# Last expert pair of layer 1: sent rows added ahead of w3, w2 tiles loaded and multiplied in halves

## Chip, cores and metric

The kernel runs on one core of a Trainium2 chip. The metric is the device time of one execution in microseconds (us); lower is better. Three runs of the kernel before the change took 819.95, 822.08 and 824.09 us, median 822.08 us.

## What is computed

One step of a two-layer network on 256 tokens (128 of a prompt, 128 of a sample) of width 1024, all in float32. What matters here is the mixture of experts that ends each layer, and that of layer 1 above all, which ends the program but for a final norm:

```python
def hierarchical_moe(h, w_grp, w_exp, w1, w3, w2):      # 16 experts, two for each token
    ...                                                 # gate: the token's weight for each expert
    hg = jnp.einsum('td,edf->tef', t, w1)               # w1, w3: 1024 x 512 for each expert
    hu = jnp.einsum('td,edf->tef', t, w3)
    a = jax.nn.silu(hg) * hu * gate[..., None].astype(t.dtype)
    y = jnp.einsum('tef,efd->td', a, w2)                # w2: 512 x 1024
    return y.reshape(b, n, d)
# then x = x + gate2 * y, and after layer 1 the outputs are rmsnorm(x, final_g)
```

## The kernel before

**Pairs of experts.** The 16 experts of a layer are taken in `PAIRS` = 8 pairs, i = 0 to 7. The rows that were routed to a pair are gathered, up to `CAP` = 64 for each expert, so that one matmul instruction for expert 2i fills output partitions 0 to 63 and one for expert 2i+1 fills 64 to 127; two such instructions run side by side. On TensorE (`compact` of the tensor block) a pair goes: w1 into PSUM bank 6, w3 into bank 7, the product silu(w1) * w3 made by VectorE (line 1747), four 128x128 transposes of it (line 807), the transposed halves copied back to SBUF by ScalarE (line 1202, `hidT_lo`) and VectorE (line 1756, `hidT_hi`), and w2 into banks 4 and 5. w2 runs with h, the half of the 1024 output columns, outside and f, the four blocks of 128 of the hidden size, inside.

**Where a pair's output goes.** In layer 1 the first `SENT` = 6 pairs are sent: their rows are scaled by the gate and scattered by GpSimd into a DRAM buffer `yrows` (line 1417), which holds two rows of 4 KB for each token. After pair 5's rows are sent, GpSimd loads `yrows` back (line 1455) with four transfers of 512 KB each, in the order group 0 first copy, group 0 second copy, group 1 first copy, group 1 second copy; the two of group g raise the semaphore `y_back[g]`. They land in the SBUF place of the tile ("w3", 1, 13), pair 6's, as soon as TensorE is done with it. VectorE adds the two copies of a group (`sum_sent(g)`, line 1710), and TensorE adds the sum to the accumulators in PSUM banks 0 to 3 by eight 128x128 matmuls against the identity (`add_sent(g)`, 16 records in the trace, as each float32 matmul is recorded as two). Pairs 6 and 7 aren't sent; their w2 output is multiplied with a scatter matrix into the same accumulators (16 records of 128x256).

**The end of pair 7 before the change.** TensorE's order is w1, w3, `add_sent(0)`, the transposes, `add_sent(1)`, w2, scatter. VectorE's order is `spread` (line 1731), `sum_sent(0)`, the product (line 1747, two halves), `sum_sent(1)`, `hidT_hi`, and the copy of the second half of the output (line 1769). Each engine runs its list in order, so an instruction that waits holds back all behind it. After the scatter come the residual, the final norm, the transposes back and the stores.

**Weights.** An expert's w1, w3 or w2 is one tile of 2 MB, 16 KB contiguous for each of 128 partitions. SyncE issues the loads in one fixed order on one queue (line 480), each as soon as the place is free, into nine places (six of `ring`, and `spare`, `bench`, `back`). For pair 7: w1 goes to a ring place and `back`, w3 to `spare` and `bench`, w2 to two ring places. The `yrows` loads go on GpSimd's queue, and both queues share the same transfer engines.

Of the kernel before, what the change touches and what calls it, by code (L numbers as in the profile page):

```python
# [29 lines left out]
FC = FF // P  # L30
# [33 lines left out]
CAP = 64  # L64
# [81 lines left out]
def backbone(nc, x_prompt, x_sample, cache_k, cache_v, c, c_ctx, w_ada, b_ada, norm_mix_g, norm_ffn_g,  # L146
# [3 lines left out]
    with ExitStack() as ctx:  # L150
# [3 lines left out]
        def sem(name):  # L154
            return ctx.enter_context(nc.semaphore(name))
# [125 lines left out]
        icnt = cst[:, C_CNT:C_CNT + 4 * P].rearrange("p (w t) -> p w t", w=4)  # L281

        slot_full = [sem(f"slot_full{s}") for s in range(SLOTS + 3)]
        tiles_used = sem("tiles_used")
        s_x = sem("s_x")
        s_cst = sem("s_cst")
# [124 lines left out]
        def landed(eng, key):  # L411

            n = TILE[key]
            eng.wait_ge(slot_full[SLOT[n]], 16 * TURN[n])
# [25 lines left out]
        def is_sent(l, i, r):  # L440

            return l == 1 and r == 0 and i < SENT

        def ysel_count(l, i, r):

            n = i + l * PAIRS
            return 2 * n - (min(i, SENT) if l == 1 and r == 0 else 0)
# [6 lines left out]
        @block.sync  # L454
        def _(sp):
            def load(key):
                n = TILE[key]
                src = SOURCE[key[0]](key[1], key[2])
                rows, width = src.shape
                dst = place(n)[:, 0:rows // P * width].rearrange("p (k n) -> p k n", k=rows // P)  # L460
                if BEFORE[n] is not None:
                    sp.wait_ge(tiles_used, BEFORE[n] + 1)
                sp.dma_start(dst, src.rearrange("(k p) n -> p k n", p=P)).then_inc(slot_full[SLOT[n]], 16)  # L463

            for g, x in enumerate((x_prompt, x_sample)):
                sp.dma_start(xtok[:, g, :], x[0]).then_inc(s_x, 16)

            sp.wait_ge(small_issued, 2)
            for key in STREAM[:TILE["w1", 0, 0]]:
                load(key)  # L470

            def load_experts(l):
                first = TILE["w1", l, 0]

                def expert_tile(i, t, expert):

                    n = first + SLOTS * i + t
                    dst = place(n).rearrange("p (k n) -> p k n", k=FC if t >= 4 else DC)
                    src = (moe_w1, moe_w3, moe_w2)[t // 2][l, expert].rearrange("(p k) n -> p k n", p=P)
                    sp.dma_start(dst, src).then_inc(slot_full[SLOT[n]], 16)  # L480

                for i in range(PAIRS):
                    for t in range(SLOTS):
                        n = first + SLOTS * i + t
                        if BEFORE[n] is not None:
                            sp.wait_ge(tiles_used, BEFORE[n] + 1)
                        elif SLOT[n] == BENCH and l == 0:

                            sp.wait_ge(pv_done, 1)
                            sp.wait_ge(s_out, 32)  # L490
                        elif SLOT[n] == SPARE:

                            sp.wait_ge(pool_done, 1)
                        elif SLOT[n] == BENCH:

                            sp.wait_ge(dconv_done, len(PE_CHUNKS))
                        else:

                            sp.wait_ge(htok_ready, 4 * l + 4)
                        expert_tile(i, t, 2 * i + t % 2)  # L500

            load_experts(0)
            for key in STREAM[TILE["w2", 0, NE - 1] + 1:TILE["w1", 1, 0]]:
                load(key)
            load_experts(1)
            for g, y in enumerate((y_prompt, y_sample)):
                for h in range(2):
                    sp.wait_ge(out_ready[2 * g + h], 1)
                    sp.dma_start(y[0][:, h * TW:(h + 1) * TW], xtok[:, g, h * TW:(h + 1) * TW]).then_inc(s_out, 16)

            sp.wait_ge(s_out, 96)
# [3 lines left out]
        def _(pe):  # L515
# [202 lines left out]
            def tile_landed(l, i, j):  # L718

                landed(pe, STREAM[TILE["w1", l, 0] + SLOTS * i + j])  # L720

            def gather(which, i, half):

# [28 lines left out]
            def compact(l, i, r):  # L752
# [5 lines left out]
                for w, bank, j in ((w1, 6, 0), (w3, 7, 2)):  # L758
                    tile_landed(l, i, j)
                    tile_landed(l, i, j + 1)  # L760
                    if j == 0:

                        pe.wait_ge(hsel_lo[r], n + 1)
                        pe.wait_ge(mod_taken, (6, 9)[l])
                    else:

                        pe.wait_ge(spread_ready[r], n + 1)
                    for k in range(DC):
                        if j == 0 and k == 4:

                            pe.wait_ge(hsel_hi[r], n + 1)
                            pe.wait_ge(pick_ready[r], n + 1)
                            for g in range(2):
                                if is_sent(l, i, r):
                                    last = mm(ps[:, 7, 0:4].rearrange("p (s u) -> p s u", s=2), pick[i % 2][:, g, :],
                                              send[:, g, :, 2 * i:2 * i + 2], g == 0, g == 1)
                                else:
                                    last = nc.tensor.transpose(ps[:, 7, g * TG:(g + 1) * TG], pick_gate[:, g, :], ident)  # L778
                            last.then_inc(spread_done[r], 1)
                        for u in range(2):  # L780
                            c = slice(CAP * u, CAP * u + CAP)
                            last = mm(ps[c, bank, :], hsel[:, k, c], w[u][:, k, :], k == 0, k == DC - 1)
                        if k == 0 and j == 2 and r == 0:

                            pe.wait_ge(hid_done[r], n * 2 + 1)
                            pe.sem_inc(tiles_used, 2)
                    last.then_inc(hid_done[r], 1)

                if ahead:

                    pe.wait_ge(rows_in, 16 * (i + l * FETCHED + 1))
                    pe.wait_ge(ysel_lo[0], n)
                    turn_rows(0)
                    if i + 2 < PAIRS:
                        pe.wait_ge(ysel_hi[0], n)
                        locate(l, i + 2, ps[:, 5, 0:1])
                elif r == 0 and l == 1:
                    add_sent(0)
                for f in range(FC):
                    if f == 2 and r == 0:  # L800

# [9 lines left out]
                if ahead:  # L811

                    pe.wait_ge(at_ready, min(i + 2, FETCHED) + l * FETCHED)
                    pe.wait_ge(ysel_hi[0], n)
                    turn_rows(1)
                elif r == 0 and l == 1:
                    add_sent(1)
                tile_landed(l, i, 4)
                tile_landed(l, i, 5)
                for h in range(2):  # L820
                    if ahead:

                        pe.wait_ge((hsel_lo, hsel_hi)[h][0], n + 2)
                    for f in range(FC):
                        if h == 0 and f % 2 == 0:

                            pe.wait_ge((hidT_lo[r], hidT_hi[r])[f // 2], n + 1)
                        for u in range(2):
                            c = slice(CAP * u, CAP * u + CAP)
                            last = mm(ps[c, 4 + h, :], hidT[:, f, c], w2[u][:, f, h * 512:(h + 1) * 512],  # L830
                                      f == 0, f == FC - 1)
                    if h == 0 or not is_sent(l, i, r):
                        last.then_inc(ysel_done[r], 1)
                    else:

                        last.then_inc(tiles_used, 2)
# [52 lines left out]
            def crowded(l, i):  # L889

                n = i + l * PAIRS
                with nc.body(f"pe_crowded_{n}", parent=pe_at[n], valid_engines=[mybir.EngineType.PE]):

                    pe.wait_ge(ysel_lo[0], n)
                    pe.wait_ge(ysel_hi[0], n)
                    way = pe.value_load(path[0:1, i:i + 1], min_val=0, max_val=2)
                    with pe.If(way == 1):
                        pe.wait_ge(more_ready, n + 1)
# [560 lines left out]
        def _(dve):  # L1459
# [247 lines left out]
            def sum_sent(g):  # L1707

                dve.wait_ge(y_back[g], 32)
                V.tensor_tensor(back_rows[:, 0, g, :], back_rows[:, 0, g, :], back_rows[:, 1, g, :],  # L1710
                                ALU.add).then_inc(y_summed, 1)

            def compact(l, i, r):
# [26 lines left out]

                if l == 1 and r == 0 and i == PAIRS - 1:
                    sum_sent(0)
                dve.wait_ge(sil_ready[r], n + 1)
                dve.wait_ge(hid_done[r], n * 2 + 2)
                for h in range(2):
# [4 lines left out]
                                    ALU.mult).then_inc(hid_ready[r], 1)  # L1750
                if r == 0 and i + 2 < PAIRS:
                    take_at(l, i + 2, ps[:, 5, 0:1])
                if l == 1 and r == 0 and i == PAIRS - 1:
                    sum_sent(1)
                dve.wait_ge(turn_done[r], n * 2 + 2)
                V.tensor_copy(hidT[:, 2:4, :], ps[:, 7, 0:2 * P].rearrange("p (f j) -> p f j", f=2)).then_inc(
                    hidT_hi[r], 1)
# [268 lines left out]
```

## Time and profile before

| | us |
|---|---|
| median of 3 runs | 822.08 |
| span of the profiled execution, first to last instruction | 821.7 |
| TensorE busy in it | 760.8 (93%) |
| VectorE / ScalarE / GpSimd busy | 235.0 / 165.6 / 50.2 |
| HBM read | 285.63 MB, 358 GB/s over the span |

The profile gives no time for the profiled execution beyond its span, which is 0.4 us under the median of the runs. The chain that ended last is TensorE for 75% of the span and DMA for 16%. Times below are us from the span's start. "issue" before a matmul is time in which the profile shows no releaser for the wait; a matmul that waits for a weight tile can appear so.

### The profile page before, as it was taken

The page shows a single profiled execution, that of the slowest core. Times are in us where ns is not written, and L with a number is a line of the kernel's source. Part 1 is how long each engine was busy: PE and PEld are TensorE (multiplying, and loading weights), DVE is VectorE, ACT ScalarE, POOL GpSimd, SP SyncE. Part 2 cuts the span into 40 slices and gives each one's busy share as a digit, 9 for nine tenths or more (in the row PEclk, how much of TensorE's full clock was granted, in tenths as well). Part 3 has the DMA queues.
Part 4 walks back from the last instruction along what each step waited for, and adds up shares of the span by engine and source line. Part 5 has one row for each costly group of instructions (what it writes and reads, how often), then busy time and mean ns, then how long its engine had stood idle before and what let it go on. Part 6 is the DMA issues. An engine that isn't in the chain of part 4 may idle for free.

```text
span 821.7 us, 10485 instructions
## 1 busy us (share of the span) xinstructions
PE 760.8 (93%) x4071; PEld 426.7 (52%) x4071; DVE 235.0 (29%) x667; ACT 165.6 (20%) x373; POOL 50.2 (6%) x74
## 2 busy tenths in 40 slices
PE   4699889999999999999799999999998989999796
PEld 4387458754344434443488758683334353333344
DVE  2301331531111111011779931451211112121115
ACT  3210420330100010001502862451010000110012
POOL 5023000010000000000100000001000000001000
PEclk9899999889999999999999999969998999999988
DMA  9997999879999999999995259577999909999941
GB/s 293 400 398 256 412 409 430 345 284 427 424 427 426 426 429 425 426 427 413 398 399 228 108 216 429 194 298 313 430 422 424 392 18 424 428 428 427 419 172 55
DMA packets 42643, 289.67 MB, mean 353 GB/s; under 512 B 4418, under 2 KB 5902, under 8 KB 30291
## 3 DMA queue, kind: packets, MB, share of 16 engines
q1 hardware_dynamic: 36752, 275.78, 81.9%
q0 software_dynamic: 5056, 11.98, 3.9%
q10 hardware_dynamic: 770, 1.06, 0.4%
q8 instruction: 39, 0.64, 0.3%
q14 instruction: 26, 0.21, 0.1%
HBM read 285.63 MB, written 8.52 MB: 358 GB/s over the span
## 4 chain that ended last, share of the span: by engine, by line
PE 75%; DMA 16%; issue 3%; DVE 3%; ACT 1%; SPq 1%; POOL 1%; PEld 0%; DVEq 0%; PEldq 0%; POOLq 0%
PE ps L517 71%; DMA ring<-in_conv_w 4%; DMA back<-in_moe_w 4%; DMA spare<-in_moe_w 3%; DMA ring<-in_w_in_ab 3%; DMA ring<-in_w_ada 3%; DVE work L1747 1%; SPq L463 1%; PE ps L939 1%; PE ps L807 1%; PE ps L741 1%; DVE rstd L1484 0%; PE ps L778 0%; POOL work L1365 0%; PE ps L669 0%
## 5 line engine op out<-in xcount | busy, mean ns | idle before, releaser
L517 PE MATMUL ps<-ring,work 128*64 128x512 f32 x1088 | 304.5, 595 | 3.0 <-issue 2.0
L517 PEld LDWEIGHTS ps<-ring,work 128*64 128x64 f32 x1088 | 94.6, 137 | 144.9 <-issue 144.8
L517 PE MATMUL ps<-back,ring 128*128 128x256 f32 x656 | 148.3, 388 | 6.3 <-DMA ring<-in_conv_w 2.6
L517 PEld LDWEIGHTS ps<-back,ring 128*128 128x128 f32 x656 | 125.7, 194 | 28.1 <-issue 4.2
L517 PE MATMUL ps<-bench,work 128*64 128x512 f32 x208 | 96.1, 611 | 2.0 <-DVE work L1704 1.4
L517 PE MATMUL ps<-spare,work 128*64 128x512 f32 x176 | 80.4, 611 | 4.7 <-issue 4.7
L517 PE MATMUL ps<-back,work 128*64 128x512 f32 x160 | 72.0, 597 | 0.0
L1747 DVE TENSOR_TENSOR work<-work,ps 128x256 f32<-128x256 f32 x34 | 19.4, 611 | 162.9 <-PE ps L517 162.9
L517 PE MATMUL ps<-ring,csil 128*32 128x512 f32 x352 | 44.4, 633 | 8.1 <-DMA ring<-in_w_ada 8.1
L1911 DVE SCALAR_TENSOR_TENSOR work<-work,dw 128x256 f32<-128x256 f32 x120 | 50.8, 479 | 1.0
L1198 ACT ACTIVATE work<-ps 128x512 f32<-128x512 f32 x17 | 10.1, 597 | 200.8 <-PE ps L517 200.8
L517 PEld LDWEIGHTS ps<-bench,work 128*64 128x64 f32 x208 | 27.8, 140 | 29.0 <-issue 28.7
L517 PEld LDWEIGHTS ps<-spare,work 128*64 128x64 f32 x176 | 24.3, 141 | 34.3 <-issue 34.3
L517 PE MATMUL ps<-work 128*128 128x256 f32 x176 | 40.9, 386 | 0.0
L517 PEld LDWEIGHTS ps<-work 128*128 128x128 f32 x176 | 32.6, 190 | 12.9 <-issue 8.9
L1191 ACT ACTIVATE work<-ps 128x512 f32<-128x512 f32 x18 | 10.8, 597 | 121.6 <-PE ps L741 97.0
L1431 POOL DMA_INDIRECT part<-hbuf,row_at x14 | 14.4, 1026 | 298.4 <-PE ps L741 274.6
L517 PE MATMUL ps<-work,xtok 128*128 128x128 f32 x128 | 22.1, 346 | 8.2 <-issue 5.1
L517 PEld LDWEIGHTS ps<-back,work 128*64 128x64 f32 x160 | 20.8, 137 | 16.7 <-issue 16.7
L1769 DVE COPY work<-ps 128x512 f32<-128x512 f32 x11 | 7.6, 691 | 74.3 <-PE ps L517 74.3
L517 PEld LDWEIGHTS ps<-ring,csil 128*32 128x32 f32 x352 | 11.9, 113 | 32.0 <-issue 19.5
L517 PE MATMUL ps<-back,ones 128*128 128x256 f32 x96 | 24.6, 408 | 3.8 <-ACT back L1111 2.2
(238 smaller groups left out, 636.4 us busy)
## 6 DMA issues: line engine op xcount, KB each, us to landing
ring<-in_moe_w SPq DMA_DIRECT2D x63, 2048.0 KB, 19.3
ring<-in_w_ada SPq DMA_DIRECT2D x22, 2048.0 KB, 18.3
bench<-in_moe_w SPq DMA_DIRECT2D x12, 2048.0 KB, 20.5
spare<-in_moe_w SPq DMA_DIRECT2D x11, 2048.0 KB, 20.6
back<-in_moe_w SPq DMA_DIRECT2D x10, 2048.0 KB, 21.8
ring<-in_conv_w SPq DMA_DIRECT2D x6, 2048.0 KB, 24.3
ring<-in_w_in_ab SPq DMA_DIRECT2D x2, 2048.0 KB, 25.0
ring<-in_w_out_ab SPq DMA_DIRECT2D x2, 2048.0 KB, 21.2
```

Of the source, the lines that this page charges most:

```text
L463: sp.dma_start(dst, src.rearrange("(k p) n -> p k n", p=P)).then_inc(slot_full[SLOT[n]], 16)
L517: return nc.tensor.matmul(out, lhsT, rhs, start=start, stop=stop, skip_group_check=True)
L741: last = nc.tensor.transpose(ps[:, 4 + half, (k % 4) * P:(k % 4 + 1) * P], hrows[:, k * P:(k + 1) * P], ident)
L807: last = nc.tensor.transpose(ps[:, 6 + f // 2, (f % 2) * P:(f % 2 + 1) * P], hid[:, f * P:(f + 1) * P], ident)
L939: last = nc.tensor.transpose(ps[:, 2 * g + k // 4, (k % 4) * P:(k % 4 + 1) * P], hT[:, k, g * TG:(g + 1) * TG], ident)
L1191: nc.scalar.activation(hsel[:, 0:4, :], ps[:, 4, :].rearrange("p (k j) -> p k j", k=4), ACT.Copy).then_inc(hsel_lo[which], 1)
L1198: nc.scalar.activation(sil, ps[:, 6, :], ACT.Silu).then_inc(sil_ready[r], 1)
L1431: nc.gpsimd.indirect_dma_start(hrows, None, hbuf[l], IndirectOffsetOnAxis(ap=row_at[:, 0:1], axis=0), bounds_check=NT - 1, oob_is_err=Fals ...
L1747: V.tensor_tensor(hid[:, h * 2 * P:(h + 1) * 2 * P].rearrange("s (f p) -> s f p", f=2), sil.rearrange("s (p f) -> s f p", f=FC)[:, f, :], ...
L1769: V.tensor_copy(ysel[:, 512:1024], ps[:, 5, :]).then_inc(ysel_hi[r], 1)
L1911: V.scalar_tensor_tensor(out=cv[k], in0=upad[:, k, :, t:t + TG], scalar=dw[:, k, t:t + 1], in1=cv[k], op0=ALU.mult, op1=ALU.add).then_inc( ...
```

## The change

- `w2` of pair 7 of layer 1 is loaded as two half tiles each: the first half (f = 0, 1) of both tiles with semaphores of their own (`front_full`), then the second halves, four transfers of 1 MB in place of two of 2 MB. Each partition's piece is 8 KB.
- `w2` of that pair is multiplied with f outside and h inside: f = 0 and 1 wait for the first halves only, f = 2 for the second. The number of matmuls is the same; both halves h of the output are now complete only in the last of the four blocks f.
- `add_sent(0)` and `add_sent(1)` stand right behind w1, ahead of w3, on TensorE; `sum_sent(1)` stands right behind `sum_sent(0)` on VectorE, ahead of the product.
- Two waits are added to the `crowded` branch, which no pair takes in this trace.

```diff
-                def expert_tile(i, t, expert):
+                def expert_tile(i, t, expert, half=None):
...
+                    if half is None:
+                        sp.dma_start(dst, src).then_inc(slot_full[SLOT[n]], 16)
+                    else:
+                        f = slice(half * FC // 2, (half + 1) * FC // 2)
+                        sp.dma_start(dst[:, f, :], src[:, f, :]).then_inc(
+                            slot_full[SLOT[n]] if half else front_full[t - 4], 16)
...
-                        expert_tile(i, t, 2 * i + t % 2)
+                        expert_tile(i, t, 2 * i + t % 2, 0 if in_halves(l, i) and t >= 4 else None)
+                    if in_halves(l, i):
+                        for t in (4, 5):
+                            expert_tile(i, t, 2 * i + t % 2, 1)
...
                     last.then_inc(hid_done[r], 1)
+                    if j == 0 and r == 0 and l == 1 and not ahead:
+                        add_sent(0)
+                        add_sent(1)
...
-                elif r == 0 and l == 1:
-                    add_sent(0)
...
-                elif r == 0 and l == 1:
-                    add_sent(1)
-                tile_landed(l, i, 4)
-                tile_landed(l, i, 5)
-                for h in range(2):
+                if in_halves(l, i):
+
+                    for f in range(FC):
+                        if f % 2 == 0:
+                            pe.wait_ge((hidT_lo[r], hidT_hi[r])[f // 2], n + 1)
+                        for u in range(2):
+                            if f == 0:
+                                pe.wait_ge(front_full[u], 16)
+                            elif f == FC // 2:
+                                tile_landed(l, i, 4 + u)
+                        for h in range(2):
+                            for u in range(2):
+                                c = slice(CAP * u, CAP * u + CAP)
+                                last = mm(ps[c, 4 + h, :], hidT[:, f, c], w2[u][:, f, h * 512:(h + 1) * 512],
+                                          f == 0, f == FC - 1)
+                            if f == FC - 1:
+                                last.then_inc(ysel_done[r], 1)
+                else:
+                    tile_landed(l, i, 4)
+                    tile_landed(l, i, 5)
+                for h in () if in_halves(l, i) else range(2):
...
                 if l == 1 and r == 0 and i == PAIRS - 1:
                     sum_sent(0)
+                    sum_sent(1)
...
-                if l == 1 and r == 0 and i == PAIRS - 1:
-                    sum_sent(1)
```

## Rows read from the trace of the kernel before

**Rows 1.** Chain of waits from 735 us: start, us, what.
```profile
739.15 29.88 DMA back<-in_moe_w
...
773.15 3.58 PE ps L517 x16
776.73 4.75 issue
781.48 11.81 PE ps L517 x48
```

**Rows 2.** Windows: stretch, length, busy us of each engine (records), TensorE clock, DMA, GB/s.
```profile
776.80:781.40 4.60, 0.00 (x0) 0.00 (x0) 0.00 (x0) 0.57 (x1) 0.00 (x0) 0.87 1.01 427
781.40:787.00 5.60, 5.52 (x14) 1.91 (x16) 0.00 (x0) 0.00 (x0) 0.00 (x0) 0.50 1.03 434
787.00:791.30 4.30, 4.30 (x21) 1.31 (x17) 0.00 (x0) 0.00 (x0) 0.00 (x0) 1.00 0.42 179
```

**Rows 3.** Weight loads of pair 7: SyncE issues (timeline), KB and us to landing (DMA view).
```profile
747.56 0.33 SPq L480 DMA_DIRECT2D bench<-in_moe_w  x1
bench<-in_moe_w SPq DMA_DIRECT2D x1, 2048.0 KB, 33.8
755.42 0.33 SPq L480 DMA_DIRECT2D ring<-in_moe_w  x1
ring<-in_moe_w SPq DMA_DIRECT2D x1, 2048.0 KB, 36.3
```

**Rows 4.** The four `yrows` loads: issues, landing of all four, median of the last two.
```profile
755.69 2.17 POOL L1455 DMA_DIRECT2D ring<-yrows  x4 [13.86 <-PEq L803]
DMA to landing us min/median/max: 10.6/20.0/28.8
ring<-yrows POOLq DMA_DIRECT2D x2, 512.0 KB, 26.0
```

**Rows 5.** Timeline of the sums on VectorE, the second add and w3's end on TensorE.
```profile
773.60 1.22 DVE L1710 TENSOR_TENSOR ring<-ring 128x1024 f32<-128x1024 f32 x1
792.48 1.22 DVE L1710 TENSOR_TENSOR ring<-ring 128x1024 f32<-128x1024 f32 x1
793.85 2.02 PE L517 MATMUL ps<-cst,ring 128*128 128x128 f32 x16
790.70 0.59 PE L517 MATMUL ps<-spare,work 128*64 128x512 f32 x1
```

**Rows 6.** Queues: packets, MB, share from 766 to 772; packets of the whole page.
```profile
q1 hardware_dynamic: 139, 2.03, 80.1%
q0 software_dynamic: 138, 0.50, 21.0%
...
DMA packets 42643, 289.67 MB, mean 353 GB/s; under 512 B 4418, under 2 KB 5902, under 8 KB 30291
```

**Rows 7.** Matmuls at full and half clock (timeline), and a stretch at half clock (windows).
```profile
757.39 7.09 PE L517 MATMUL ps<-ring,work 128*64 128x512 f32 x32 [0.65 <-issue]
782.36 1.06 PE L517 MATMUL ps<-spare,work 128*64 128x512 f32 x1
783.21 1.06 PE L517 MATMUL ps<-spare,work 128*64 128x512 f32 x1
538.97 3.65 PE L939 MATMUL ps<-cst,back 128*128 128x128 f32 x16
39.50:43.00 3.50, 3.38 (x8) 2.76 (x9) 0.00 (x0) 3.50 (x13) 0.00 (x0) 0.51 1.05 384
```

**Rows 8.** Pair 6 between w3 and w2 (timeline): VectorE's product, ScalarE's copy.
```profile
754.67 1.14 DVE L1747 TENSOR_TENSOR work<-work,ps 128x256 f32<-128x256 f32 x2 [10.55 <-PE ps L517]
755.82 0.38 ACT L1202 ACTIVATE work<-ps 128x256 f32<-128x256 f32 x1
```

**Rows 9.** Pair 7's output (timeline): ScalarE's first copy, TensorE's scatter.
```profile
799.50 0.60 ACT L1212 ACTIVATE work<-ps 128x512 f32<-128x512 f32 x1 [5.58 <-PE ps L517]
802.82 3.72 PE L517 MATMUL ps<-work 128*128 128x256 f32 x16
```

More of the change, by code:

```diff
@@ L283, in backbone @@
         slot_full = [sem(f"slot_full{s}") for s in range(SLOTS + 3)]
+        front_full = [sem(f"front_full{u}") for u in range(2)]
         tiles_used = sem("tiles_used")
@@ L442, in is_sent, with in_halves @@
             return l == 1 and r == 0 and i < SENT
+        def in_halves(l, i):
+            return l == 1 and i == PAIRS - 1
         def ysel_count(l, i, r):
@@ L479, in expert_tile @@
                     src = (moe_w1, moe_w3, moe_w2)[t // 2][l, expert].rearrange("(p k) n -> p k n", p=P)
-                    sp.dma_start(dst, src).then_inc(slot_full[SLOT[n]], 16)
+                    if half is None:
[4 more added lines that the diff above has]
+                            slot_full[SLOT[n]] if half else front_full[t - 4], 16)
                 for i in range(PAIRS):
@@ L720, in tile_landed @@
                 landed(pe, STREAM[TILE["w1", l, 0] + SLOTS * i + j])
+                if in_halves(l, i) and j >= 4:
+                    pe.wait_ge(front_full[j - 4], 16)
             def gather(which, i, half):
@@ L895, in crowded @@
                     pe.wait_ge(ysel_hi[0], n)
+                    pe.wait_ge(hsel_lo[0], n + 1)
+                    pe.wait_ge(hsel_hi[0], n + 1)
                     way = pe.value_load(path[0:1, i:i + 1], min_val=0, max_val=2)
```

## The prediction, made before the changed kernel was run

> **What bounds the kernel now.** I read the chain of waits first, since the change touches only the last pair. There the reader sees four facts [rows 1]. TensorE's w1 of pair 7 starts when the tile in `back` lands at 739.15 + 29.88 = 769.03; it ends at 773.15 + 3.58 = 776.73; then TensorE stands for 4.75 us; from 781.48 it runs without a stop worth naming to the end of w2. The chain calls the 4.75 us "issue", so I looked up what w3 needs: its second tile goes to `bench`, issued at 747.56 and landed 33.8 us later, at 781.36 [rows 3]. So w3 starts 0.12 us after its weights are home, and the stall is a transfer, not TensorE.
>
> The windows view shows a second cost of that stall [rows 2]. The transfer engines are full through it (427 GB/s, then 434), so nothing loads faster by being asked for earlier. And the granted clock falls in it: the mean is 0.87 over the idle stretch and 0.50, the 1.2 GHz level, from 781.40 to 787.00, then 1.00 again, 2.4 GHz. w3 therefore runs its first 5.5 us at half clock and ends at 790.70 + 0.59 = 791.29 [rows 5], 9.8 us after its start, where 32 records of the same shape took 7.09 us in pair 6 at full clock [rows 7].
>
> w2 is not held by its weights. Its last tile was issued at 755.42 and landed 36.3 us later, at 791.7 [rows 3]; w2 starts where `add_sent(1)` ends, at 793.85 + 2.02 = 795.87 less the overlap of pipelined matmuls, 795.80. Between w3's end and w2's start lie 4.5 us, of which two adds of some 2 us each are the larger part.
>
> **The sent rows decide.** The adds can go into the 4.75 us stall only if their data are there. VectorE's first sum starts at 773.60, so group 0 is home by then. Of group 1 the kernel before tells nothing by a wait, since its sum comes at 792.48 [rows 5]. The DMA view does. Four loads are issued from 755.69 on, over 2.17 us, so at about 755.7, 756.2, 756.8 and 757.3; the first lands after 10.6 us, the last after 28.8, and the last two have a median of 26.0, so 23.2 for the third [rows 4]. That puts the landings at 766.3, about 773.1, 780.0 and 786.1. `y_back[1]` needs the fourth: **786.1, some 4.7 us after w3's weights**. After the change TensorE may not start w3 before it has added group 1.
>
> **Part by part.**
>
> *`add_sent(0)` ahead of w3.* Its sum ends at 773.60 + 1.22 = 774.8, before w1 ends. It runs from about 776.8 to 778.8, in a stall that exists anyway: nothing on the path.
>
> *The second sum and `add_sent(1)` ahead of w3.* VectorE waits for the fourth load; queued behind it there are only the product and the copies, which need w3 anyway. Does the fourth load land when it did? From 766 to 772 the two queues moved 139 and 138 packets, with 2.03 and 0.50 MB [rows 6]: packet for packet, where a packet of GpSimd's queue is mostly one 4 KB row. On SyncE's queue it is a whole 16 KB partition: the page counts 42643 - 30291 = 12352 packets of 8 KB and more, and 96 expert tiles of 128 partitions are 12288 [rows 6]. The change halves the packets of w2, the tiles that follow `bench` at 781.4, so one turn of both queues is 8 + 4 = 12 KB in place of 20, 0.6 of the time. At 781.4 the fourth load has had 1.4 of its 6.1 us (780.0 to 786.1); 0.77 x 6.1 x 0.6 = 2.8 us more give 784.2, and with the 6.8 us that the transfers before it took, 784.7. I take 784.4. Bounds: 783.7 if the whole load runs beside halves (6.1 x 0.6), 786.1 if the queues share by bytes and nothing changes.
>
> The Trainium skill, page "DMA: Bandwidth & Descriptors", section "Queues, rings and completion order", says that a transfer engine takes turns between its queues packet by packet. The counts of 139 and 138 agree; by that rule the fourth load comes early, as I take it, and without it the sum would be that of rival 1.
>
> Then 1.22 us of sum and about 0.15 to start TensorE, as from 792.48 + 1.22 = 793.70 to 793.85 [rows 5]: it starts at 785.8, after 7 us of idling. A stall of 4.75 us took the clock to half [rows 2], so `add_sent(1)` runs at half clock. Sixteen such 128x128 records at half clock took 3.65 us [rows 7], at full 2.02 [rows 5]; I take 3.7, and w3 starts at 789.5. The full-clock price would need a stall without a fall, which no row here shows for 7 us.
>
> *w3.* It started at 781.48, so it is 8.0 us late. Part comes back: the half clock lasted 5.5 us from the restart [rows 2], and if it does so again it ends at 791.3. A pair of records costs 0.85 us at half clock (782.36 to 783.21) and 7.09 / 16 = 0.44 at full, 0.43 without the tail of the last [rows 7]. The 1.8 us from 789.5 take 2.1 of the 16 pairs, 13.9 x 0.43 = 6.0 the rest, and 0.16 the last one's tail: w3 ends at 797.4, 6.1 later than 791.3. The half clock is bounded below by 3.5 us, a stretch after an earlier stall that ran at a mean of 0.51 throughout [rows 7], and above by a longer one, as the next restart may fall differently: -0.9 and +0.6 us.
>
> *From w3 to w2.* With the adds gone, the way is that of pair 6: product at 754.67, ScalarE's copy ends at 755.82 + 0.38 = 756.20 [rows 8], 0.05 for TensorE to see it, and the product itself starts 0.1 after w3's end; together 1.75 us in place of 4.5. **This returns 2.75.** `hidT_hi` is done some 0.6 us after w2's start and is asked for only at f = 2, half of 7.0 us later.
>
> *w2 in halves.* Now w2 starts at 799.2. Both tiles were home at 791.7 and the bytes are the same, so the halves, front and back, are home some 7 us before they are needed: loading and multiplying by halves gives nothing on this path, and the two further issues on SyncE hide behind a queue that is full. The matmuls are the same in number and shape, 795.80 to 802.82, 7.0 us. It costs a little: h = 0 is complete only in the last block f, 0.86 us before the end, where ScalarE's copy used to run at 799.50, 3.3 us before the scatter [rows 9]. The copy takes 0.60, so about 0.1 us shows.
>
> *Sum.* 797.4 + 1.75 + 7.0 + 0.1 = 806.3 for the scatter's start in place of 802.82: **+3.5 us**. All behind it stays. The profiled execution would go from 821.7 to 825.2; the median of the runs lies 0.4 above the span, so I predict **825.6 us** (+0.4%). Checked the other way: 6.1 - 2.75 + 0.1 = 3.5.
>
> **Rivals.**
>
> 1. *Shares by bytes.* If packets of half the size change nothing, the fourth load lands at 786.1, TensorE restarts at 787.5, and all is 1.7 us later: +5.2, 827.3. For it: only whole tiles are shown in the trace. Against it: the even packet counts.
>
> 2. *The rows come in time, and the change is faster.* If the fourth load were home by 781.48 - 2.0 - 0.15 - 1.22 = 778.1, both adds would fill the stall; if the clock then stays up, w3 would take 781.48 to 788.5, and the scatter would start at 788.5 + 1.75 + 7.1 = 797.4: -5.4, 816.7. The point of no gain is a landing at 780.9. For it: the landings are read from the DMA view alone, and nothing in the kernel before waits for the fourth. Against it: the third lands at 780.0 and four times 0.5 MB at the pace of rows 6 cannot come sooner.
>
> 3. *A short half clock.* If it lasts 3.5 us from the restart, w3 runs at full clock: -0.9, 824.7. If the clock doesn't fall at all, add and w3 cost 1.7 and 0.9 less, 823.0.
>
> 4. *The change doesn't do what it says:* that w2 is bound by its load and the halves free it. The row of the last tile (791.7 against 795.80) speaks against it; it would matter only in rival 2, where w2 would start at 790.3 and need its second half at 793.8, still later than 791.7.
>
> **How the numbers follow.** Forecast 0.53, rival 1 0.21, rival 2 0.12, rival 3 0.14; rival 4 has no time of its own. The forecast's own range is 824.7 to 826.9. The range reaches from rival 3's lower time, less 1 us since three runs of one kernel spread by 4 us, to rival 1 and 0.7 above it: 822.0 to 828.0, which leaves out rival 2 and some tails. A measurement of this kernel can tell about 0.5%, 4.1 us, from no change; slower by more starts at 826.2, within the forecast's range. Slower: rival 1 and a third of the forecast, 0.39. Faster: 0.12 and a little for noise, 0.13. Same: 0.48.
>
> **What would show it.** Right: in the changed profile the second sum on VectorE starts at about 784.4, long after the first; `add_sent(1)` starts at about 785.8 with 16 records over some 3.7 us at clock 0.50; w3 starts at about 789.5, though its weights land at 781.4 as before; from w3's end to w2's start there are 1.75 us; the page counts about 256 packets more. The load's landing tells the forecast (784.4) from rival 1 (786.1). Wrong: a second sum before 781, w3 starting with its weights, or w2 waiting for its halves.

## The result: 0.65% slower, and the profile after

The changed kernel took 827.57 us (median of 14 runs, 823.36 to 829.56) against 822.15 of the kernel before it: ratio 1.0065, 95% interval 1.005 to 1.0081. That is slower, by 5.4 us where 4.1 were called measurable; the interval begins just at that half per cent. The time is inside the predicted range (822.0 to 828.0) and 2 us above the predicted 825.6. Here and below ratios use fast runs alone, as a few executions (one of 1122 us among them) fall into a slower state, and they need not be the exact quotient of the two medians.

The page of the changed kernel: span, and packets of all queues.

```profile
span 827.4 us, 10490 instructions
DMA packets 42931, 289.68 MB, mean 350 GB/s; under 512 B 4449, under 2 KB 5933, under 8 KB 30322
```

Its span is 5.7 us longer than before's 821.7. The profiled execution took 829.29 us, 1.9 above its span and 1.7 above the median; in the profiled runs of the experiments, too, the time lies 1.8 to 1.9 us above the span, so before's profile, too, is of an execution slower than its median (estimate: 823.5 us). The page counts 288 packets more than before [rows 6]; 256 of them are the halves.

Pair 7 in the timeline of the changed kernel (start, us, engine, line, tiles out<-in, count, and in brackets the idle time before it with its releaser): w1's first matmul, the two sums on VectorE with the adds on TensorE, w3's first and last, the product, w2, the scatter.

```profile
772.90 0.61 PE L530 MATMUL ps<-ring,work 128*64 128x512 f32 x1 [1.14 <-DMA back<-in_moe_w]
...
777.38 1.22 DVE L1744 TENSOR_TENSOR ring<-ring 128x1024 f32<-128x1024 f32 x1
...
780.44 2.05 PE L530 MATMUL ps<-cst,ring 128*128 128x128 f32 x16
787.13 1.22 DVE L1744 TENSOR_TENSOR ring<-ring 128x1024 f32<-128x1024 f32 x1 [8.54 <-DMA ring<-yrows]
788.50 3.75 PE L530 MATMUL ps<-cst,ring 128*128 128x128 f32 x16 [6.01 <-DVE ring L1744]
792.19 1.05 PE L530 MATMUL ps<-spare,work 128*64 128x512 f32 x1
...
799.08 0.59 PE L530 MATMUL ps<-spare,work 128*64 128x512 f32 x1
799.80 1.12 DVE L1782 TENSOR_TENSOR work<-work,ps 128x256 f32<-128x256 f32 x2 [11.45 <-PE ps L530]
801.37 7.09 PE L530 MATMUL ps<-ring,work 128*64 128x512 f32 x32
808.39 3.72 PE L530 MATMUL ps<-work 128*128 128x256 f32 x16
```

The stall before w3 is now named: TensorE idles 6.01 us for VectorE's second sum, and VectorE had idled 8.54 us for `yrows`. The DMA view (first line: KB and us from issue to landing) and the view of the loads' own line (second) put w3's own weights ahead of that:

```profile
bench<-in_moe_w SPq DMA_DIRECT2D x1, 2048.0 KB, 33.9
...
DMA to landing us min/median/max: 10.7/20.0/26.4
```

The tile in `bench` was issued at 751.21 and landed 33.9 us later, at 785.1. The second line is that of the four `yrows` loads, issued from 759.1 to 760.7: the fourth landed 26.4 us after its issue, at 787.1, just when the second sum starts. TensorE takes w3 up only at 792.19, 7.1 us after w3's weights are home. The clock in the windows view of that stretch (third column from the right), before, in and after the restart:

```profile
784.00:786.00 2.00, 0.00 (x0) 0.00 (x0) 0.00 (x0) 0.00 (x0) 0.00 (x0) 1.00 1.03 422
786.00:788.00 2.00, 0.00 (x0) 0.00 (x0) 0.86 (x1) 0.00 (x0) 0.00 (x0) 0.55 1.00 414
788.00:790.00 2.00, 1.50 (x7) 1.53 (x8) 0.36 (x1) 0.00 (x0) 0.00 (x0) 0.50 1.02 426
790.00:792.00 2.00, 2.00 (x11) 1.96 (x10) 0.00 (x0) 0.00 (x0) 0.00 (x0) 0.50 1.01 422
792.00:794.00 2.00, 2.00 (x10) 0.64 (x10) 0.00 (x0) 0.00 (x0) 0.00 (x0) 0.74 0.74 311
```

The add runs at 1.2 GHz, 3.7 us where the first add took 2.05, and w3 at 2.4 GHz from about 793.0 on.

**Where the 5.7 us lie.** I split each profile at w1 of pair 7 and at the scatter, and call what lies between them the tail. Before: 769.13 to 802.82, 33.69 us. After: 772.90 to 808.39, 35.49 us. So the tail gives only 1.8 of the 5.7; 3.8 were lost before w1 of pair 7, where the prediction had put nothing; 0.1 lies behind the scatter. The split is that of two single executions.

**An error in what stands ahead of the prediction.** There I wrote that no pair takes the `crowded` branch, to which the change adds two waits. That is wrong: TensorE's first matmuls of pair 3 of layer 1 in the trace of before (timeline) lie in it. They gather that pair's rows, once at 627 and once at 662 us:

```profile
627.48 4.84 PE L517 MATMUL ps<-work,xtok 128*128 128x128 f32 x21 [3.40 <-issue]
632.75 1.70 PE L517 MATMUL ps<-work,xtok 128*128 128x128 f32 x11 [0.43 <-issue]
...
662.69 3.81 PE L517 MATMUL ps<-work,xtok 128*128 128x128 f32 x32 [1.32 <-issue]
```

The same in the kernel after:

```profile
626.93 3.35 PE L530 MATMUL ps<-work,xtok 128*128 128x128 f32 x14 [3.38 <-issue]
631.56 4.00 PE L530 MATMUL ps<-work,xtok 128*128 128x128 f32 x18 [1.28 <-issue]
...
665.63 5.44 PE L530 MATMUL ps<-work,xtok 128*128 128x128 f32 x32 [2.90 <-issue]
```

From the first gather to w1 of pair 7 it is 141.65 us before and 145.97 after. The second gather alone is idle 1.6 us longer and takes 1.6 longer. The prediction has no term for any of this.

### The profile page after: what moved, and what is told of

Same layout as the page of the kernel before. It is cut to its first block, busy times and chain, and to the rows that moved or that the text cites. A ratio compares the mean times of both kernels' runs of the same rounds, so it can differ in the third digit from the quotient of the medians.

```text
span 827.4 us, 10490 instructions
## 1 busy us (share of the span) xinstructions
PE 766.5 (93%) x4071; PEld 432.2 (52%) x4071; DVE 235.3 (28%) x667; ACT 165.8 (20%) x373; POOL 50.2 (6%) x74
## 4 chain that ended last, share of the span: by engine, by line
PE 78%; DMA 12%; DVE 3%; issue 3%; POOL 1%; ACT 1%; SPq 1%; PEld 0%; DVEq 0%; PEldq 0%; POOLq 0%
PE ps L530 74%; DMA ring<-in_conv_w 4%; DMA ring<-yrows 3%; DMA ring<-in_w_in_ab 3%; DMA ring<-in_w_ada 3%; DVE work L1782 1%; PE ps L973 1%; SPq L468 1%; PE ps L823 1%; PE ps L756 1%; PE ps L793 0%; DVE rstd L1518 0%; POOL work L1399 0%; PE ps L682 0%; DVE back L1980 0%
## 5 line engine op out<-in xcount | busy, mean ns | idle before, releaser
L530 PE MATMUL ps<-bench,work 128*64 128x512 f32 x208 | 94.0, 599 | 1.5 <-DVE work L1738 1.4
L530 PE MATMUL ps<-spare,work 128*64 128x512 f32 x176 | 78.0, 596 | 0.0
L530 PE MATMUL ps<-work,xtok 128*128 128x128 f32 x128 | 24.9, 376 | 10.6 <-issue 7.6
L530 PEld LDWEIGHTS ps<-work,xtok 128*128 128x128 f32 x128 | 23.6, 285 | 12.1 <-issue 12.1
L530 PEld LDWEIGHTS ps<-back,work 128*64 128x64 f32 x160 | 20.8, 137 | 16.7 <-issue 16.7
```

What stands on the lines that cost most here:

```text
L530: return nc.tensor.matmul(out, lhsT, rhs, start=start, stop=stop, skip_group_check=True)
```

## The experiments

There were three theories to tell apart; more than one can hold. **A**: the cost is in pair 7, because group 1's rows land after w3's weights and TensorE has to add them first. **B**: the two waits in the `crowded` branch cost time by being executed. **C**: code that is longer shifts the branch's instructions, and the branch, entered by a jump, is fetched worse from its new place. A fourth question was whether the halves of w2 do anything. Times below are medians, each run with the kernel before on the same chip (three chips in all), and ratios are to that kernel.

**Each part alone.** `adds_only` is the kernel before with sums and adds moved ahead, w2 whole, no new waits:

```diff
                     last.then_inc(hid_done[r], 1)
+                    if j == 0 and r == 0 and l == 1 and not ahead:
+                        add_sent(0)
+                        add_sent(1)
...
-                elif r == 0 and l == 1:
-                    add_sent(0)
...
-                elif r == 0 and l == 1:
-                    add_sent(1)
...
                     sum_sent(0)
+                    sum_sent(1)
...
-                if l == 1 and r == 0 and i == PAIRS - 1:
-                    sum_sent(1)
```

> Both adds and both sums ahead, w2 loaded and multiplied whole, no added waits. The sums wait for the last load of the sent rows. My prediction's theory (queues share packet for packet, so halves of w2 bring that load 1.7 us sooner): here it lands 30.4 us after the first of the four was issued, as before, so the time is 1.7 us above the changed kernel's end of pair 7. From w1's start to the scatter's start before 33.7 us, after 35.5; here 37 to 38.5. Rival (shares by bytes): 35.5 as after, landing 28.0 us after the first issue. Time of the whole: 825 to 829; by theory B of the waits run it is free of the branch's cost, so under 827.

It took 826.95 us, ratio 1.0059 (1.0032 to 1.0086). `halves_only` is the kernel after with the opposite edit to this one and without the two waits:

```diff
-                        add_sent(0)
-                        add_sent(1)
...
+                elif r == 0 and l == 1:
+                    add_sent(0)
...
+                elif r == 0 and l == 1:
+                    add_sent(1)
...
-                    pe.wait_ge(hsel_lo[0], n + 1)
-                    pe.wait_ge(hsel_hi[0], n + 1)
...
-                    sum_sent(1)
...
+                if l == 1 and r == 0 and i == PAIRS - 1:
+                    sum_sent(1)
```

> w2 of pair 7 loaded and multiplied in halves, adds and sums where they were before, no added waits. Prediction: nothing gained, as w2's weights are home 4 us before w2 starts: 33.7 us from w1's start to the scatter's start, 822.2 +- 1. Packet for packet: the last load of the sent rows lands about 28 us after the first was issued (before 30.4); by bytes 30.4. Rival (halves bring something of their own): 821 or less.

It took 824.38 us, ratio 1.0014 (0.9992 to 1.0036). The third is `waits_only`, the kernel before with the waits alone:

```diff
                     pe.wait_ge(ysel_lo[0], n)
                     pe.wait_ge(ysel_hi[0], n)
+                    pe.wait_ge(hsel_lo[0], n + 1)
+                    pe.wait_ge(hsel_hi[0], n + 1)
```

> The kernel before with nothing but the two added waits in the branch for a crowded pair. In the profile of the changed kernel pair 3 of layer 1 goes through that branch, and w1 of pair 7 starts 3.8 us later than in the kernel before (772.90 against 769.13), of which the branch adds most. Theory A (the time is all made in pair 7): 822, no change, and w1 of pair 7 starts at 769 +- 1. Theory B (the branch's code, with its waits or its place in the instruction stream, costs time too): 823 to 826, and the stall ahead of the second gather of pair 3 is 2.9 us as after the change, not 1.3 as before.

It took 824.32 us, ratio 1.0032 (1.0013 to 1.0051). So the loss comes apart into two: the adds' order, 4.8 us by its ratio, and the waits, 2.6, with intervals that overlap; the halves by themselves gain nothing. The profile of `waits_only` shows its loss nowhere: it is of the fastest of its twelve runs (821.60 us), w1 of pair 7 starts at 768.38, and the second gather waits 1.15 us, not the 2.9 that was expected. In `adds_only` (timeline: w1, the second sum, the second add, the scatter) group 1 decides even more, since here w2's packets are whole:

```profile
768.85 0.61 PE L517 MATMUL ps<-ring,work 128*64 128x512 f32 x1 [0.99 <-DMA back<-in_moe_w]
...
785.39 1.22 DVE L1709 TENSOR_TENSOR ring<-ring 128x1024 f32<-128x1024 f32 x1 [10.86 <-DMA ring<-yrows]
786.76 3.75 PE L517 MATMUL ps<-cst,ring 128*128 128x128 f32 x16 [8.33 <-DVE ring L1709]
...
806.79 3.72 PE L517 MATMUL ps<-work 128*128 128x256 f32 x16
```

The tail is 37.94 us, 2.45 longer than that of after. In the view of the loads' line the fourth load lands 28.5 us after its issue here, 28.8 in the kernel before, 26.4 in after and 26.3 in `halves_only`. In all seven kernels that load w2 whole and the rows as before it takes 28.5 to 28.8, in all four with halves 26.3 or 26.4. Here is the line of `adds_only`, then the two queues of the kernel after from 783 to 785 (packets, MB, share of the engines):

```profile
DMA to landing us min/median/max: 10.4/19.7/28.5
```

```profile
q1 hardware_dynamic: 71, 0.56, 66.8%
q0 software_dynamic: 67, 0.27, 33.1%
```

So halves do what the prediction said of packets: they bring the other queue's load home some 2.3 us sooner. Packets of 8 KB and of 4 KB take turns almost one for one, as those of 16 and 4 KB did before [rows 6]. That is the rule of the Trainium skill named there (turns packet by packet), and the counts and the landings agree with it; sharing by bytes would have changed nothing.

**What the prediction costed, exactly.** `no_waits` is the kernel after without the two waits in the branch, so all that the prediction's sum holds and nothing else:

```diff
-                    pe.wait_ge(hsel_lo[0], n + 1)
-                    pe.wait_ge(hsel_hi[0], n + 1)
```

> The changed kernel without the two added waits in the branch for a crowded pair: adds and sums ahead, halves, nothing else. The waits alone cost 2.6 us (ratio 1.0032). Theory B (the branch costs part of the change's time, through its waits): 823.5 to 825, ratio to the kernel before 1.002 to 1.004, and from the first gather of pair 3 to w1 of pair 7 under 144 us (after 146.0, before 141.7). Theory C (the branch's cost comes from where its code lies, which the halves move too): 825 to 828 with a second gather that waits 2.5 to 2.9 us and three instruction fetches around it, as in all kernels with halves so far. From w1's start to the scatter's start in pair 7: 34.4 to 36, as in the changed kernel.

It took 825.96 us against 822.23, ratio 1.0042 (1.0014 to 1.0070): by its ratio +3.5 us, with an interval from 1.2 to 5.8, where the sum said +3.5. Timeline of its second sum, second add and scatter:

```profile
782.34 1.23 DVE L1742 TENSOR_TENSOR ring<-ring 128x1024 f32<-128x1024 f32 x1 [8.67 <-DMA ring<-yrows]
783.71 3.75 PE L530 MATMUL ps<-cst,ring 128*128 128x128 f32 x16 [6.15 <-DVE ring L1742]
...
803.76 3.72 PE L530 MATMUL ps<-work 128*128 128x256 f32 x16
```

With w1 at 767.98 its tail is 35.78, that of after (35.49) within 0.3. Theory A stands for pair 7. That the ratio meets the sum is in part luck: the tail is only 2.1 us longer than before's. The time lies above the 823.5 to 825 expected by theory B, while from the first gather to w1 it is 141.96 us, as B has it.

**Only the first add ahead.** If group 1 is what costs, the change with group 1 left in its old place should keep the gain of `add_sent(0)` in the stall. `first_add` is the kernel after with this edit:

```diff
                         add_sent(0)
-                        add_sent(1)
...
+                elif r == 0 and l == 1:
+                    add_sent(1)
...
                     sum_sent(0)
-                    sum_sent(1)
...
+                if l == 1 and r == 0 and i == PAIRS - 1:
+                    sum_sent(1)
```

> As the changed kernel, but only group 0 is added ahead of w3; group 1 is summed and added where it was before. If the cost is the wait for the last load of the sent rows, w3 starts with its weights again, 12.4 us after w1's start, and one add of 2.05 us has left the way from w3 to w2, so the scatter starts 31.5 to 32 us after w1's start where w3 still runs its first 5.5 us at half clock, and 29 if the clock stays up: 817 to 820.5, plus what the branch costs by theory B. If it is the reordering as such that costs, it stays near 825.

It took 823.90 us, ratio 1.0036 (1.0013 to 1.0058). The loss in the tail is gone, but the expected gain is not there. The timeline shows why:

```profile
782.87 0.90 PE L530 MATMUL ps<-spare,work 128*64 128x512 f32 x1 [2.80 <-issue]
...
791.76 1.12 DVE L1782 TENSOR_TENSOR work<-work,ps 128x256 f32<-128x256 f32 x2 [15.60 <-PE ps L530]
792.80 1.22 DVE L1745 TENSOR_TENSOR ring<-ring 128x1024 f32<-128x1024 f32 x1
794.16 2.02 PE L530 MATMUL ps<-cst,ring 128*128 128x128 f32 x16 [0.79 <-DVE ring L1745]
...
803.13 3.72 PE L530 MATMUL ps<-work 128*128 128x256 f32 x16
```

TensorE's second add waits for VectorE's second sum, and that stands behind the product, as in the kernel before [rows 5]. The first add used to run while VectorE was busy with that; moving it only lengthens TensorE's wait later. From w3's end to w2's start it is 4.5 us, as before. The tail, 32.65 us from w1 at 770.48, misses the 31.5 to 32 expected, though w3 ran only 3.4 us at half clock, and is like that of kernels that leave pair 7's order alone with as short a half clock (last section). The ratio holds the two waits too.

**Waits or place?** Four kernels set B against C. `pad4` and `pad24` are the kernel before with 4 or 24 more waits on a semaphore already raised, at the end of TensorE's main program, ahead of the branch's code; `dead24` has 24 in the branch of layer 0's first pair, which is not taken, so that they shift code and never run; `waits_back` is `waits_only` with 488 in that same branch. The edits of `pad24` and of `dead24`:

```diff
+            for _ in range(24):
+                pe.wait_ge(hsel_lo[0], 1)
             last_bb = nc.cur_bb
             pe.br("pe_end")
```

```diff
+                    for _ in range(24 if n == 0 else 0):
+                        pe.wait_ge(hsel_lo[0], 1)
                     pe.wait_ge(ysel_lo[0], n)
```

> The kernel before with four waits that are long fulfilled put at the end of TensorE's program, ahead of the code of the crowded branches: no new wait in any branch, only their code lies four instructions later. Theory C: the gathers of pair 3 break at another place, the second waits up to 2.9 us and three fetches of instructions lie around it, and the time is 1 to 3 us above the kernel before. If only waits inside the branch cost: no change, 822 +- 1, second gather after 1.2 to 1.6 us.

> As the run before with 24 such waits, as many as the two added waits in each of the twelve branches up to pair 3 of layer 1. Theory C: as the kernel with the waits alone: the first gather breaks after some 15 records, not 21, and the time is 2 to 3 us above the kernel before. If waits inside the branch cost as such: no change, 822 +- 1.5.

> The kernel before with 24 waits in the branch of layer 0's first pair, which isn't taken: nothing more is executed, but the code of all later branches lies as much later as two added waits in each would put it. Where the first gather of pair 3 breaks tells the shift: 21 records before, 15 in the kernel with the waits and in the one with 24 waits at the end. Theory C (place of the code): break after 15, and the time 1.5 to 3 us above the kernel before, as theirs (1.0032 and 1.0025). Theory B (executed waits): break after 15, and no change, 822 +- 1.2.

> The two waits in every branch, and 488 more in the branch that isn't taken, so that the code lies later by some 256 instructions in all; if instructions come in blocks of that many, the first gather breaks after 21 records again. Theory C: with the break back at 21 the time is back at 822 +- 1.2 although the waits are executed. Theory B: the waits still cost 2 to 3 us. If the break is elsewhere, the run tells only that place's time.

Ratios: `pad4` 1.0009 (0.9985 to 1.0034), `pad24` 1.0025 (1.0000 to 1.0050), `dead24` 1.0007 (0.9979 to 1.0035), `waits_back` 1.0018 (0.9992 to 1.0045). The first gather of the branch in `waits_only`, then in `dead24`, then in `waits_back` (timeline):

```profile
625.24 3.56 PE L517 MATMUL ps<-work,xtok 128*128 128x128 f32 x15 [3.56 <-issue]
630.23 3.79 PE L517 MATMUL ps<-work,xtok 128*128 128x128 f32 x17 [1.42 <-issue]
```

```profile
626.57 3.56 PE L517 MATMUL ps<-work,xtok 128*128 128x128 f32 x15 [3.46 <-issue]
...
```

```profile
625.86 6.59 PE L517 MATMUL ps<-work,xtok 128*128 128x128 f32 x32 [3.38 <-issue]
```

The break in the gather follows the place of the code: after 21 records in before, 15 in `waits_only`, `pad24` and `dead24`, 14 in after and `first_add`, 20 in `pad4`, and none that shows in `waits_back`. So C describes where the gather breaks. But what it costs does not come out: `dead24`, which breaks where `waits_only` does, lost nothing that can be measured, and all intervals overlap. Nor does C explain the second gather, which took 5.44 us after 2.46 to 2.90 us of idling in after, `halves_only` and `first_add`, and 3.81 after 1.49 in `no_waits`, which has the code of the halves too. In the profiles, one execution each, it is from the first gather to w1 of pair 7 146.0 and 146.2 us in after and `first_add`, which have both halves and waits; 143.1 and 141.7 in `waits_only` and `waits_back`, which have the waits; and 141.1 to 143.8 in the seven kernels without the waits that load the rows as before, the highest of them `dead24`. So neither the waits alone nor a later place alone shows as many as the 4.3 us that after has over before. **Whether the waits cost by running, by their place or only together with the halves stays open**; that `waits_only` was slower than before by 0.1 to 0.5% is measured.

**Rows later, adds last.** If group 1's rows come too late to be added ahead of w3, and if they share the transfer engines with w3's weights, then the other direction should gain: let GpSimd load them only once w3 has landed, and add them behind w2. `late_rows` is the kernel after, without the two waits, with this:

```diff
             pool.wait_ge(y_sent, 16 * SENT)
+            landed(pool, ("w3", 1, NE - 1))
...
-                    if j == 0 and r == 0 and l == 1 and not ahead:
-                        add_sent(0)
-                        add_sent(1)
...
                 pe.wait_ge(y_zeroed, l + 1)
+                if r == 0 and l == 1 and not ahead:
+                    add_sent(0)
+                    add_sent(1)
                 pe.wait_ge(ysel_lo[r], n + 1)
```

On VectorE both sums move behind the copy `hidT_hi`:

```diff
-                    sum_sent(0)
-                    sum_sent(1)
...
+                if l == 1 and r == 0 and i == PAIRS - 1:
+                    sum_sent(0)
+                    sum_sent(1)
```

> Halves as in the change, no added waits, but the sent rows are loaded only once w3 of pair 7 is home, and summed and added behind w2. If it is the sent rows' 2 MB, sharing the transfer engines with the weights, that make w3 late and TensorE idle (4.75 us before), then w3's second tile lands some 4.5 us sooner, the stall all but goes, the clock stays up, and both adds run behind w2: scatter at 28 to 30 us after w1's start in place of 33.7, and w1 itself up to 1 us sooner: 815 to 818. If the adds then wait for the rows (last row home after w2's end): 818 to 821.

It took **817.24 us against 822.23, ratio 0.9937 (0.9913 to 0.9962)**: faster than the kernels before and after. Timeline: w1, w3 after a stall of 1.30 us, the front half of w2, the sums, the back half, the adds, the scatter; then the windows view of w3.

```profile
765.99 0.64 PE L530 MATMUL ps<-ring,work 128*64 128x512 f32 x1
...
774.90 0.61 PE L530 MATMUL ps<-spare,work 128*64 128x512 f32 x1 [1.30 <-issue]
...
783.67 3.65 PE L530 MATMUL ps<-ring,work 128*64 128x512 f32 x16
787.25 1.22 DVE L1743 TENSOR_TENSOR ring<-ring 128x1024 f32<-128x1024 f32 x1 [3.08 <-DMA ring<-yrows]
787.77 3.65 PE L530 MATMUL ps<-ring,work 128*64 128x512 f32 x16 [0.45 <-DMA ring<-in_moe_w]
...
791.36 3.84 PE L530 MATMUL ps<-cst,ring 128*128 128x128 f32 x32
795.03 3.62 PE L530 MATMUL ps<-work 128*128 128x256 f32 x16
```

```profile
775.00:781.00 6.00, 6.00 (x30) 2.41 (x32) 0.00 (x0) 0.00 (x0) 2.17 (x4) 1.00 1.01 418
```

The `bench` tile lands 29.3 us after its issue in place of 33.8 [rows 3], since the rows' packets are not between its own. The stall falls from 4.75 to 1.30 us, and the clock stays at 1.00. Tail: 29.04 us. What the later rows and the later adds give each by itself was not run.

Are the halves of use here, where w2 is now what the transfers bring last? `late_whole` is the same edit made to the kernel before, so that w2 stays in whole tiles; its timeline has w3, w2, the adds and the scatter:

> Sent rows loaded once w3 of pair 7 is home and added behind w2, but w2 loaded and multiplied whole. With halves this order took 817.2 (ratio 0.9937), and w2's first half ran before the last half was home (it waited 0.45 us at half way). If the halves are worth something once the sent rows are out of w3's way, w2 starts 3 to 5 us later here, when its last tile is home, some 21 us after w1's start, and the time is 819 to 822. If they are worth nothing here either: 817 +- 1.

```profile
774.44 0.61 PE L517 MATMUL ps<-spare,work 128*64 128x512 f32 x1 [1.29 <-issue]
...
785.68 9.99 PE L517 MATMUL ps<-ring,work 128*64 128x512 f32 x32 [2.41 <-DMA ring<-in_moe_w]
795.60 3.84 PE L517 MATMUL ps<-cst,ring 128*128 128x128 f32 x32
799.27 3.62 PE L517 MATMUL ps<-work 128*128 128x256 f32 x16
```

It took 820.90 us against 822.89, ratio 0.9982 (0.9955 to 1.0008), no measured gain. w2 waits 2.41 us for its whole tiles and then runs partly at half clock (granted clock 0.50 from 784.8 to 791.4), 9.99 us for what takes 7.1 at full. Its tail, 33.72 us, is that of before. Set against 0.9937 the halves are worth about 3.7 us here, by the tails 4.7; the two runs' intervals overlap by a hair, and the runs are from two chips.

## Why the prediction came out as it did

The tail alone, step by step, each time counted from w1's start so that what was lost earlier doesn't enter (predicted from 769.13, measured in the kernel after from 772.90):

| step | predicted | after |
|---|---|---|
| second sum starts (fourth load home) | 15.3 | 14.2 |
| `add_sent(1)` starts | 16.7 | 15.6 |
| w3 starts | 20.4 | 19.3 |
| w3 ends | 28.3 | 26.8 |
| w2 starts | 30.0 | 28.5 |
| scatter starts | 37.2 | 35.5 |

- **What bounds it, right.** TensorE waits for the fourth row load, not for its weights; the order of the landings read from the DMA view (w3's weights, then group 1) was as read, and w3 starts with its weights long home.
- **The landing: right mechanism, size off by 1.0 us.** Halves bring the load sooner. Against w3's weights it was 4.7 us late before, 3.0 predicted, 2.0 measured (787.1 against 785.1). That is even 0.3 below the bound of 783.7, which was 2.3 late. The sum let the halves begin only when `bench` is home; in the kernel after the weight packets are down to 8 KB in the mean from 783 on, 2 us before that. (For a transfer of 6.8 us the prediction's own working gives 784.6, not 784.7, which changes nothing.) Rival 1, sharing by bytes, is refuted by 26.3 and 26.4 against 28.5 to 28.8 us.
- **The add at half clock, right:** 3.69 us from its start to w3's, predicted 3.7.
- **Half clock in w3, too long by 0.4 us.** From the restart at 788.50 to 793.0 it lasted 4.5 us, not 5.5; inside the bounds that the sum gave. Of rival 3, the half clock was shorter, but by 1.0 and not 2.0 us, and the clock did fall.
- **From w3 to w2, right:** 799.67 to 801.37 is 1.70 us, predicted 1.75. w2 took 7.02, predicted 7.0. The 0.1 us for the late copy did not show.
- **Halves of no use on this path, right:** `halves_only`, 1.0014 with 1 inside, and a tail of 32.61 us beside 32.56 to 32.62 in three kernels with w2 whole. Rival 4 falls with it. Once the rows are out of the way its case does come about: w2 waits 0.45 us for its second halves in `late_rows` and 2.41 for its whole tiles in `late_whole`. The prediction had left room for that in rival 2 alone.
- **Rival 2, the rows in time:** not in the changed kernel; `late_rows` gains about the 5 us named there by another way, taking the rows out of the way.
- **What the sum left out: all that lies before pair 7.** The two waits were costed at nothing because of a branch wrongly said not to be taken, and the branch lies in a stretch that was 4.3 us longer in the profile after. The kernel without them lost 3.5 us, with them 5.4, and `waits_only` lost 2.6; this fits, but the intervals overlap, and the runs do not show how the time is lost.

So the mechanism of the tail was right, and its size was not: the tail came out 1.8 us longer than before, or 2.4 against the mean of the kernels that keep its order (last section), where the sum said 3.5. The two errors, a tail forecast too long and nothing for what comes before it, have opposite signs, so that the total came within 2 us and inside the range partly by luck. "Within 0.5%" was given a little more chance than "slower", and what came before pair 7 moved the kernel over that line.

## What to carry to other kernels

Before moving work into a stall, find when its inputs land, from issue plus landing time, and compare with the end of the stall: here group 1 came 4.7 us after that end, 2.0 after w3's weights even with halves, and the stall grew. If the inputs share the transfer engines with the load that makes the stall, try them later, not earlier: that gave 0.6% here, together with halves of w2, and nothing that could be measured without them. A branch is taken or not by what the trace shows on its lines, and shape and count of the matmuls there tell it; look before a term is set to zero.

## What was not expected of the hardware

**The same stall, two prices.** Seven kernels keep the old order of adds, and all have the stall before w3, 4.73 to 4.76 us long. But the half-clock stretch at its end is not always of one length. In the windows view of before it runs from 780.2 to 787.0, 6.8 us; in `waits_only` it is 3.4, and begins only 0.4 us after the restart (timeline of its restart, then windows):

```profile
780.71 0.65 PE L517 MATMUL ps<-spare,work 128*64 128x512 f32 x1 [4.73 <-issue]
```

```profile
782.00:784.00 2.00, 2.00 (x8) 0.89 (x6) 0.00 (x0) 0.00 (x0) 0.00 (x0) 0.50 1.04 438
784.00:786.00 2.00, 2.00 (x10) 0.67 (x9) 0.00 (x0) 0.00 (x0) 0.00 (x0) 0.86 1.04 442
```

Tails are 33.6 to 33.8 us in before, `pad4` and `waits_back` (6.8 us at half clock), and 32.6 in `waits_only`, `halves_only`, `pad24` and `dead24` (3.4 us). So 1.1 us of the difference between two profiles can lie in the length of that stretch alone. Against the mean tail of the seven, 33.1, the change costs its tail 2.4 us, not the 1.8 that two profiles show.

**A jump shows as "issue".** At the entry of the `crowded` branch TensorE stands for 3.2 to 3.7 us with no releaser in all thirteen profiles, and in ten of them once more within the first gather, at a place that moves with the code. The Trainium skill, page "Runtime: NRT & Kernel Launch", section "Instruction fetch mechanics", says that a taken branch to a target that is not yet fetched waits for that fetch. The moving break agrees with it. The DMA view of before shows one packet of 0.02 MB on a queue of kind `instruction` between 624.0 and 624.5, where the 3.40 us begin, and another between 630.0 and 630.5, within the gather; that TensorE waits for them is not shown, and what the break costs the whole kernel could not be told from nothing.
